# A two-block transformer kernel on one Trainium2 core: an opening in smaller pieces, and the first feed-forward's turns taken off TensorE

## What is computed

```python
h = h + fox_mixer(rms_norm(h, mix_norm), fox_w_in, ...)
h = h + conv_ffn(rms_norm(h, ffn_norm), ffn_w_up, ffn_conv_w, ffn_conv_b, ffn_w_down)
def conv_ffn(h, w_up, conv_w, conv_b, w_down):         # w_up: 2048 x 11264, w_down: 5632 x 2048
    up = h @ w_up
    padded = jnp.pad(up, ((0, 0), (CONV_WIDTH - 1, 0), (0, 0)))
    y = conv_b + conv_w[0] * padded[:, 0:seq]
    for tap in range(1, CONV_WIDTH):
        y = y + conv_w[tap] * padded[:, tap:tap + seq]
    gate, val = jnp.split(y, 2, axis=-1)
    return (jax.nn.silu(gate) * val) @ w_down
```

## Time and profile before

| | |
|---|---|
| median of three runs | 2606.37 us |
| the profiled execution's own time | 2606.77 us |
| its span | 2604.8 us |
| TensorE busy | 2573.1 us (99%) |
| VectorE busy | 1596.4 us (61%) |
| ScalarE busy | 1248.2 us (48%) |
| GpSimd busy | 39.1 us (2%) |
| DMA engines busy | 62% with SyncE's transfers, mean 190 GB/s |

### The profile page before, as it was taken

How to read it: one execution, slowest core, us unless ns; L and a number is a source line. 1 busy time by engine, 2 the same in 40 slices (tenths; PEclk the granted TensorE clock), 3 DMA queues, 4 the chain that set the end, 5 groups by cost and what they waited for, 6 DMA issues and landing times.

```text
span 2604.8 us, 32206 instructions
## 1 busy us (share of the span) xinstructions
PE 2573.1 (99%) x11867; PEld 2141.5 (82%) x11867; DVE 1596.4 (61%) x1778; ACT 1248.2 (48%) x1586; POOL 39.1 (2%) x44
## 2 busy tenths in 40 slices
PE   7999999999999999999999999999999999999998
PEld 6888888888888888888888888888888888888886
DVE  4565555666666666675767555456556666666665
ACT  5555555545444444554343545444444444444444
POOL 0000000000000000000000000000000000000000
PEclk9999999999999999999999999999999999999999
DMA  6666555666656666656555655655577676767674
GB/s 199 219 181 174 169 164 176 198 188 187 186 185 191 185 181 186 187 182 186 160 155 164 192 171 163 181 190 186 186 224 220 211 224 213 221 210 224 208 225 157
DMA packets 259509, 495.41 MB, mean 190 GB/s; under 512 B 18060, under 2 KB 27108, under 8 KB 259300
## 3 DMA queue, kind: packets, MB, share of 16 engines
q1 hardware_dynamic: 254720, 486.60, 61.6%
q10 hardware_dynamic: 4019, 4.58, 0.5%
q0 software_dynamic: 688, 3.15, 0.4%
HBM read 483.76 MB, written 10.51 MB: 190 GB/s over the span
## 4 chain that ended last, share of the span: by engine, by line
PE 98%; ACT 0%; DVE 0%; ACTq 0%; DMA 0%; issue 0%; POOL 0%; POOLq 0%; SPq 0%
PE acc L442 31%; PE acc L444 31%; PE acc L443 31%; PE acc L455 2%; PE acc L672 1%; PE acc L515 1%; PE acc L522 0%; DMA raw<-in_w 0%; ACTq L885 0%; PE acc L532 0%; PE acc L544 0%; DVE w_lo L1221 0%; ACT w_hi L827 0%; PE acc L545 0%; PE acc L699 0%
## 5 line engine op out<-in xcount | busy, mean ns | idle before, releaser
L1221 DVE TENSOR_TENSOR w_lo<-raw,w_hi 128x1024 fp32r<-128x1024 f32 x888 | 1080.6, 1223 | 835.8 <-ACT w_hi L827 834.1
L827 ACT ACTIVATE w_hi<-raw 128x1024 fp32r<-128x1024 f32 x888 | 935.8, 1059 | 1060.1 <-PE acc L444 1038.4
L442 PE MATMUL acc<-w_hi,A_hi 128*128 128x512 f32 x1952 | 772.3, 396 | 2.2 <-ACT scratch L837 1.1
L444 PE MATMUL acc<-w_hi,A_lo 128*128 128x512 f32 x1952 | 761.2, 390 | 0.0
L443 PE MATMUL acc<-w_lo,A_hi 128*128 128x512 f32 x1952 | 761.0, 390 | 0.0
L444 PEld LDWEIGHTS acc<-w_hi,A_lo 128*128 128x128 f32 x1952 | 366.9, 188 | 77.2
L442 PEld LDWEIGHTS acc<-w_hi,A_hi 128*128 128x128 f32 x1952 | 367.2, 188 | 76.5 <-issue 1.7
L443 PEld LDWEIGHTS acc<-w_lo,A_hi 128*128 128x128 f32 x1952 | 367.3, 188 | 73.1
L442 PE MATMUL acc<-w_hi,B_hi 128*128 128x512 f32 x800 | 313.6, 392 | 1.5 <-ACT scratch L1181 1.5
L444 PE MATMUL acc<-w_hi,B_lo 128*128 128x512 f32 x800 | 311.5, 389 | 0.0
L443 PE MATMUL acc<-w_lo,B_hi 128*128 128x512 f32 x800 | 311.3, 389 | 0.0
(11 more groups left out here) (160 smaller groups left out, 1095.3 us busy)
## 6 DMA issues: line engine op xcount, KB each, us to landing
raw<-in_up SPq DMA_DIRECT2D x304, 512.0 KB, 4.5
raw<-in_w SPq DMA_DIRECT2D x272, 512.0 KB, 4.0
raw<-in_down SPq DMA_DIRECT2D x216, 512.0 KB, 4.1
raw<-in_wo SPq DMA_DIRECT2D x64, 512.0 KB, 4.1
raw<-in_wa SPq DMA_DIRECT2D x16, 512.0 KB, 4.9
raw<-in_wb SPq DMA_DIRECT2D x16, 512.0 KB, 4.6
turn_rows<-scratch SPq DMA_DIRECT2D x16, 512.0 KB, 6.5
scratch<-turn_rows SPq DMA_DIRECT2D x64, 128.0 KB, 3.7
```

The source lines that it names most:

```text
L442: pe.matmul(o, hi[:, kt, ts], wh, start=first and kk == 0, stop=False)
L444: m = pe.matmul(o, lo[:, kt, ts], wh, start=False, stop=last and kk == SLOT_K - 1)
L827: act.activation(w_hi[:, q % RING, :], raw[:, q % RING, :], ACT.Copy).then_inc(w_hi_ready, 1)
L1221: dve.tensor_tensor(w_lo[:, q % RING, :], raw[:, q % RING, :], f32(w_hi[:, q % RING, :]), ALU.subtract).then_inc(w_lo_ready, 1)
```

## The change

**Opening.** The first chunk of x comes as two halves and slot 0's weights as two transfers of 256 KB; a small load `mix_rows` brings the first 16 gain rows apart from the other tables. TensorE turns half a chunk (`turn_pair`), begins slot 0 on it (`gemm_first`), turns the second half inside slot 0, and turns chunks 1, 2 and 3 before slots 1, 2 and 3. The other tables are turned before slot 4. ScalarE's loads of the forget gate's weights and of masks move to slots 2 and 7. Of the four broadcasts of `cum_rows` (768 KB each) three move from slots 20 to 22 of the first fox pass to slots 0, 2 and 4 of the next (`spread_gates`).

**First feed-forward.** No `turn` is left in it, 22 fewer. The evacuation writes by blocks into `up_q` (the same two instructions). VectorE transposes 32x32 blocks into `up_x` (`turn_blocks`: at slot 8, and after the split at q = 0 of the downs). GpSimd writes `up_x` to `up_rows` in DRAM, waits, and reads it back into `up_t` in four transfers. ScalarE makes one more copy, `up_t` to `up_f`, that puts the blocks in order, and both engines take the taps from `up_f`. The gate's taps move from p = 10 to p = 14. The value's stay at p = 1, but in the second pass they stand at p = 5, and at the end at q = 5 where they stood at q = 2. Down products now use banks 4 to 7 in turn; in the last eight slots banks 0 to 3 and 6, 7.

**Second feed-forward.** The first `ups2` uses banks 6 and 7 and its successor banks 0 and 1, so the wait for `up2_out` between them is gone.

```diff
-            split(0, -AHEAD)
-            operand(TN_X, A_hi, 0, G_MIX)
+            act.dma_start(mix_rows, a["rows"][0:KT, :]).then_inc(mix_in, 16)
...
+            act.wait_ge(w_early, 16)
+            early_split(0).then_inc(w0_hi, 1)
+            act.wait_ge(early_turned, 1)
+            early_operand(0).then_inc(early_hi, 1)
...
-                if 2 * SPC + 3 <= p < 2 * SPC + 3 + GROUPS:
-                    g = p - 2 * SPC - 3
+                if p == 2 * SPC + 3:
                     act.wait_ge(cum_out, 32)
+                    spread_gates(0)
...
+                        if isinstance(g, int) and p in (0, 2, 4):
+                            spread_gates(1 + p // 2)
...
-                    elif p == 1:
-                        pe.wait_ge(up1_out, 2 * i)
-                        turn(halves(stage_q), TN_FFN1 + 2 * i - 1)
-                    if p == 10:
-                        pe.wait_ge(up1_out, 2 * i + 1)
-                        turn(halves(stage_q), TN_FFN1 + 2 * i)
+                    elif p % SPC == 0:
+                        pe.wait_ge(up1_out, 2 * i - 1 + p // SPC)
...
+            def conv_tap(i, half, dst):
+                n = 2 * i + half
+                act.wait_ge(up1_back, 64 * (n + 1))
...
+                act.activation(up_f.rearrange("p (m a q) -> p m a q", m=JT * TT, a=4), from_quads(up_t),
+                               ACT.Copy).then_inc(up1_flat, 1)
+                act.wait_ge(up1_flat, n + 1)
...
-                    if p == 10:
+                    if p == 14:
...
+            ups1(R3 + U1, 1, at=5)
...
-                if q == 2:
+                if q == 5:
                     act.wait_ge(gated, FFN1 - 1)
                     conv_value(FFN1 - 1)
-                if q == 3:
+                if q == 6:
                     gated_value(FFN1 - 1, B_hi)
...
+            def turn_blocks(n, first=False):
+                dve.wait_ge(up1_out, n + 1)
+                if not first:
+                    dve.wait_ge(up1_sent, 16 * n)
+                dve.transpose(up_x, up_q).then_inc(up1_block, 1)
...
+            for n in range(2 * FFN1):
+                pool.wait_ge(up1_block, n + 1)
+                if n:
+                    pool.wait_ge(up1_back, 64 * n)
+                pool.dma_start(up_rows, up_x).then_inc(up1_sent, 16)
+                pool.wait_ge(up1_sent, 16 * (n + 1))
+                if n:
+                    pool.wait_ge(up1_flat, n)
+                for b in range(4):
+                    pool.dma_start(up_t[32 * b:32 * (b + 1), :].rearrange("p (a e) -> p a e", a=4),
+                                   up_by_quad[b]).then_inc(up1_back, 16)
```

More of the change, by code:

```diff
@@ L462, in chunk_of_resid, with turn_pair @@
                 return lambda t, j: resid[:, t, c * CW + j * P:c * CW + (j + 1) * P]
-            pe.wait_ge(ident_in, 16)
[L466 to L470, removed]
+            def turn_pair(j0, done):
+                for j in (j0, j0 + 1):
+                    for t in range(TT):
+                        m = pe.transpose(acc[:, 4 + j, t * P:(t + 1) * P], chunk_of_resid(0)(t, j), ident)
+                m.then_inc(done, 1)
@@ L799, in ups2 @@
                             pe.wait_ge(turn_dve, TN_RES2 + 4)
-                    elif p == 0:
+                    elif p == 0 and not isinstance(i, int):
                         pe.wait_ge(up2_out, i)
-                    gemm(R, p, B_hi, B_lo, p, BK[0], p == 0, p == SPC - 1)
+                    gemm(R, p, B_hi, B_lo, p, BK[3 if first else 0], p == 0, p == SPC - 1)
             ups2(R7, 0, first=True)
@@ L1320, in first_steps @@
                 if p == 2 * SPC:
+                    dve.wait_ge(const_in, 16)
                     dve.wait_ge(cum_turned, 1)
@@ L1421, in ups1, with downs @@
                         sum_squares(1)
-                    if not first and 1 <= p <= 3:
-                        value_steps(p - 1, i - 1)
-                    if p == 10:
-                        conv_taps(i, 0, g_T, TN_FFN1 + 2 * i)
+                    if not first and at <= p <= at + 2:
+                        value_steps(p - at, i - 1)
+                    if p == 14:
+                        conv_taps(i, 0, g_T)
                         dve.wait_ge(gate_sig, i + 1)
                         chain.link(dve.tensor_tensor(g_T, g_T, s_T, ALU.mult))
-            def downs(R, p0, banks, done, ahead=True, steps=None):
+                    if p == SPC:
+                        turn_blocks(2 * i, first)
+                if first:
+                    turn_blocks(1)
+            def downs(R, p0, banks, done, ahead=True, steps=None, turn=None):
                 for q in range(2 * NCH):
@@ L1432, in downs @@
                         split(R, p0 + q)
+                    if turn is not None and q == 0:
+                        turn_blocks(turn)
                     if steps:
@@ L1438, in _ @@
             ups1(R3, 0, first=True)
-            with dve.Fori(1, FFN1 - 1) as i:
-                chain.enter(i, 1, 3)
+            ups1(R3 + U1, 1, at=5)
+            downs(R3 + U1, 2 * SPC, D1_BANKS, down1_out, turn=3)
+            with dve.Fori(2, FFN1 - 1) as i:
+                chain.enter(i, 2, 3)
                 R = R3 + U1 + B3 * (i - 1)
                 ups1(R, i)
-                downs(R, 2 * SPC, D1_BANKS, down1_out)
-                chain.leave(FFN1 - 2)
+                downs(R, 2 * SPC, D1_BANKS, down1_out, turn=2 * i + 1)
+                chain.leave(FFN1 - 3)
             ups1(R4 - 2 - B3, FFN1 - 1)
-            downs(R4 - 4, 0, D1_BANKS, down1_out, steps=lambda q: value_steps(q - 2, FFN1 - 1, B_hi, B_lo))
+            downs(R4 - 4, 0, D1_BANKS, down1_out, steps=lambda q: value_steps(q - 5, FFN1 - 1, B_hi, B_lo),
+                  turn=2 * FFN1 - 1)
             def down1_steps(q):
```

227 lines of the change are left out of this document (155 added, 72 removed).

## The result

The changed kernel takes 2650.60 us (median of four runs, 2649.92 to 2652.93), the kernel before 2606.43 (four runs): a ratio of 1.0173, 95% interval 1.0155 to 1.0190. It is 44 us slower. The forecast was 2610 with a range up to 2630, so it was wrong: the time lies outside the range, and the number forecast was one that can't be told from no change. Slower had the largest single chance, 0.40, and its mechanism was rival B, with 0.24; B's price was too low. The profiled execution took 2652.93 us with a span of 2651.1.

The account below looks back on a forecast made before the run. TensorE, 98% of the chain that ended last, was taken as the bound. Gains of 30.1 us against costs of 35.3 gave 2606.8 + 5.2 = 2612.0 for the profiled execution; the forecast was 2610, range 2598 to 2630.

Parts of the forecast that it names:

- rival B: First feed-forward: the trip is long, gate data late in every pass; at 14.5 us, 23 over the sum, 2634; chance 0.24.
- The turns: First feed-forward: 22 turns at 0.91 us leave TensorE, 20.0 us gained, called sure.
- The opening: Start of the kernel: slot 8 begins 7.0 us earlier, near 37.5; between 4.5 and 8.5.
- the gates: Opening: three broadcasts leave a stretch of waits for weight loads, 1.4 us gained, between 0 and 1.5.
- the banks: Second feed-forward: `ups2` no longer waits for the evacuation of its own bank, 1.7 us gained.
- The place of the waits: First feed-forward: TensorE waits for `w_lo` at slot 18 of each pass, and for `B_lo` before the last eight slots.
- The last stall: Last value half: TensorE stands 13.7 us before the last eight slots, plus 2.5 for slow matmuls behind it.
- the trip's length: First feed-forward: write and four reads take 12.5 us where 12.7 is allowed; bounds 8 and 15, 3 us for scatter.
- no cost for slow matmuls behind short waits: First feed-forward: half-rate matmuls priced only behind the last long gap, 2.5 us; none behind short waits.
- the gate half with its data in time: Slot 18 of every pass: TensorE waits 0.75 us for `w_lo` even with data there; ends 0.4 and 1.1.
- The value half: Each pass, slot 6: margin 2.1 less 0.91 and 1.06 leaves +0.1, so no cost.
- the second pass: First feed-forward: value data 4.2 us late at p = 5 and the gate's trip behind it cost 8.6 us together.

Follow-up runs that it names:

- the run with the held load: Changed kernel with SyncE's weight load for slot 18 of each pass held until the gate half's round trip is back: 2619.96 us, ratio 1.0054.
- SyncE's: Changed kernel with the same round trips issued by SyncE on its own queue between the weight loads, not by GpSimd: 2627.76 us, ratio 1.0082.

## Why the prediction was wrong

**What held.** The turns, 20.0. The opening, 7.0 and 1.4 for the gates, measured 9.8 together; the banks, 1.7, measured 1.8. The place of the waits: slot 18 of each pass for VectorE's `w_lo`, two in the second pass, one before the last eight slots. The last stall nearly in size: 13.7 and 2.5 were forecast, 15.9 and 1.7 measured. But that is in part luck: its trip took 16.1 and not 12.5, with which the working gives 17.3 for the wait, so the chain behind it was priced 1.4 too long.

**The step that failed first: the trip's length.** "I take 12.5, so the median trip is just in time." I took it from SyncE's trips in the second feed-forward, and SyncE's trip does take 11.8 to 12.8. What I carried over with it was a state that another queue doesn't have: fewer weight loads beside the reads, because the queue that issues the loads is busy with the reads until the fourth is out. The transfers of 1 MB from GpSimd at 7.8 ran beside loads, and I gave it the far end of the range, 15; the gate half takes 14.1 and the value half 15.4. I weighed a slower wake (0.3 measured) and a slower issue, 0.55, and looked for starvation of GpSimd's issue, which there was none of (0.55 to 0.59 in all but the first, 0.74), but not for the loads. The rival with the long trip named them in half a sentence, and priced them at 23 us.

**The second: no cost for slow matmuls behind short waits.** "A gap of 1.15 cost nothing, so the short waits get none." That is true of 1.15. But the same prediction has a rival in which every wait is 2.5 or more, and there the term had to come back. It was 12.0 in six of nine passes, and 2.9 and 2.8 behind the second pass's two gaps. So the clock's term hangs on the waits and can't be left out once they are long, though it did not follow behind every long one.

**The third: the gate half with its data in time**, 0.75 a pass, is 1.15 (the run with the held load and SyncE's both show it). Two pieces of the difference are seen: the taps from SBUF take 2.08 and not 1.93, and the tap waits 0.25 for the copy's own signal where I had 0.1 for all restarts. The value half, priced at nothing with a margin of 0.1, costs 0.3.

**The fourth: the second pass**, 8.6 forecast, 18.4 measured. The value's trip took 14.8, 2.3 longer than I took it, and counts in both gaps (4.8 and 6.9), since the gate's evacuation and trip stand behind it; the gate's own trip took 15.9; and 2.9 and 2.8 are the slow rate behind the gaps.

With what was measured, 14.1 for the gate's trip (1.4 past 12.7), 1.15, 1.3 for the clock and 0.3 for a value half, the same steps give 9 x (1.15 + 1.4 + 1.3 + 0.3) = 37 for the nine passes, and with the 36 measured at the two ends 2606.8 - 31.6 + 73 = 2648 for the execution of 2652.9. The list of places was nearly complete, the value halves' 2.7 us apart; the one duration on which twelve of them hang was read from a queue in another state.

**Verdict and range.** Each microsecond of trip past 12.7 was said to cost 12 or 13 us, and both ends of the trip, 8 and 15, were in the text. At 15 that is 2640, and some 2652 with the clock's term: the range ended at 2630 although its own bound went beyond. Two sums of the text were slightly off, without weight for the result: the short end of the trip, 2.8 + 1.8 + 2.8, is 7.4 and not 8, and the sum at a trip of 12.0 is 2607 and not 2608.

## What to carry to other kernels

When a transfer is to be issued from another queue, take its duration from a transfer that ran beside the same traffic, not from one whose own queue held the other traffic back: here four reads of 128 KB took 3.1 to 3.3 us each with hardly any load beside them and 4.7 to 7.8 beside weight loads. A step that is a trip and a chain long is best given a place several slots before it is needed: moving the gate's copy and taps by four slots, with the last pass back on TensorE and the second pass's value taps two slots later, made a change that lost 44 us gain 30, although the gate's trip stayed at 13.8. And before a step is moved, look at what stands at its new place on each engine (an evacuation, an addition that frees a bank), since that wait takes the old one's place.

## What the runs showed of the hardware that I had not expected

- Reads from GpSimd's queue take 3.1 to 3.3 us (medians) while no weight load is issued, and the fourth of four 7.2 to 7.8 beside loads. In the 6 us in which four such reads were carried out beside loads, GpSimd's queue had 37% of the DMA engines' time and SyncE's 64%.
- TensorE at the lower of its two rates (granted clock 0.50, starts 0.43 us apart) for 2.7 to 5.3 us behind waits of 2.5 to 3.6 us in six of nine cases, and at full rate behind the other three, a wait of 3.51 among them. In the runs' first feed-forwards the shortest wait with a slow stretch behind it is 2.4 (by the starts, with one load held); behind waits up to 2.3 there is none. Which waits have one is not decided by their length alone, and what else decides stays open.
- GpSimd's issue of a transfer of 512 KB takes 0.56 and shows no hold-up by VectorE, which is busy 64% of the first feed-forward. The Trainium skill (SBUF — State Buffer, Who interferes with whom) names `copy`, `cast` and `tensor_scalar` as the VectorE operations that can lock GpSimd out of the shared port. VectorE runs none of these there, so its rule has no case here.
